# Four forget logits carried by the value matmuls of a fused two-block layer, in place of a weight tile of their own

## What is computed

```python
z = h @ w_in
qa, ka, va, qb, kb, vb, fz, gza, gzb = jnp.split(z, SPLIT_POINTS, axis=-1)
ya = dilated_mixture(qa, ka, va) @ w_up_a
yb = forgetting_attention(qb, kb, vb, fz, b_forget) @ w_up_b
merged = jax.nn.sigmoid(gza) * ya + jax.nn.sigmoid(gzb) * yb
return merged @ w_out

# in forgetting_attention: 4 heads of 64, so fz has 4 columns, beside vb's 256
log_f = jax.nn.log_sigmoid(f_logit + b_forget)
F = jnp.cumsum(log_f, axis=1).transpose(0, 2, 1)
s = q_t . k_s * Dh ** -0.5 + (F_t - F_s)      # causal softmax over s, then times v
```

## Time and profile before

| | us |
|---|---|
| median of 3 runs (1991.33 to 1991.41) | 1991.33 |
| the profiled execution | 1992.63 |
| its span, first to last instruction | 1990.9 |
| TensorE's matmuls busy | 1973.5 |
| TensorE's weight loads busy | 1655.7 |
| VectorE / ScalarE / GpSimd busy | 1018.7 / 695.1 / 406.8 |

### The profile page before, as it was taken

How to read it: one execution, slowest core, us unless ns; L and a number is a source line. 1 busy time by engine, 2 the same in 40 slices (tenths; PEclk the granted TensorE clock), 3 DMA queues, 4 the chain that set the end, 5 groups by cost and what they waited for, 6 DMA issues and landing times.

```text
span 1990.9 us, 27158 instructions
## 1 busy us (share of the span) xinstructions
PE 1973.5 (99%) x11044; PEld 1655.7 (83%) x11044; DVE 1018.7 (51%) x1391; ACT 695.1 (35%) x1008; POOL 406.8 (20%) x212
## 2 busy tenths in 40 slices
PE   8999999999999999999999999999999999999998
PEld 7878888888888888889888888888877888888887
DVE  5468757457345336626727535642544664322435
ACT  6357643122124323315312212534434352222222
POOL 1000007696600001000568661000000200000000
PEclk9999999999999999999999999999999999999999
DMA  6221134444333232222445442232221223323231
GB/s 190 79 64 44 44 117 148 158 149 147 129 106 117 73 108 85 85 102 91 156 138 169 148 134 100 85 94 81 71 85 64 86 84 106 104 98 106 84 106 64
DMA packets 135033, 208.91 MB, mean 105 GB/s; under 512 B 6347, under 2 KB 105865, under 8 KB 134921
## 3 DMA queue, kind: packets, MB, share of 16 engines
q1 hardware_dynamic: 125952, 180.37, 27.9%
q0 software_dynamic: 6912, 25.17, 3.8%
q10 hardware_dynamic: 2056, 1.76, 0.3%
HBM read 205.18 MB, written 2.10 MB: 104 GB/s over the span
## 4 chain that ended last, share of the span: by engine, by line
PE 94%; DVE 3%; ACT 2%; issue 0%; ACTq 0%
PE ps L2158 28%; PE ps L2160 28%; PE ps L2159 28%; PE ps L2219 1%; PE ps L2609 1%; PE ps L2212 1%; PE ps L2211 1%; PE ps L2620 1%; PE ps L2709 1%; PE ps L2182 1%; PE ps L2801 1%; DVE m L1466 0%; PE ps L2598 0%; PE ps L2597 0%; ACT ps L761 0%
## 5 line engine op out<-in xcount | busy, mean ns | idle before, releaser
L1388 DVE TENSOR_TENSOR w_lo<-w_raw,w_hi 128x2048 fp32r<-128x2048 f32 x149 | 350.9, 2355 | 577.0 <-ACT w_hi L726 577.0
L2158 PE MATMUL ps<-x_hi,w_hi 128*128 128x512 f32 x1240 | 489.1, 394 | 0.4 <-DVE w_lo L1388 0.4
L2160 PE MATMUL ps<-x_hi,w_lo 128*128 128x512 f32 x1240 | 483.0, 390 | 0.0
L2159 PE MATMUL ps<-x_lo,w_hi 128*128 128x512 f32 x1240 | 482.9, 389 | 0.0
L726 ACT ACTIVATE w_hi<-w_raw 128x2048 fp32r<-128x2048 f32 x151 | 288.9, 1913 | 536.1 <-PE ps L2160 435.1
L2158 PEld LDWEIGHTS ps<-x_hi,w_hi 128*128 128x128 f32 x1240 | 233.0, 188 | 51.0 <-issue 3.5
L2160 PEld LDWEIGHTS ps<-x_hi,w_lo 128*128 128x128 f32 x1240 | 232.7, 188 | 48.8
L2159 PEld LDWEIGHTS ps<-x_lo,w_hi 128*128 128x128 f32 x1240 | 233.1, 188 | 45.9
L2158 PE MATMUL ps<-w_hi,h_hi 128*128 128x512 f32 x688 | 267.8, 389 | 0.0
L2160 PE MATMUL ps<-w_hi,h_lo 128*128 128x512 f32 x688 | 267.7, 389 | 0.0
L2159 PE MATMUL ps<-w_lo,h_hi 128*128 128x512 f32 x688 | 267.7, 389 | 0.0
(11 more groups left out here) (404 smaller groups left out, 2694.2 us busy)
## 6 DMA issues: line engine op xcount, KB each, us to landing
w_raw<-in_ffn_w SPq DMA_DIRECT2D x64, 1024.0 KB, 5.4
ada_w<-in_w_ada POOLq DMA_DIRECT2D x48, 512.0 KB, 4.2
w_raw<-in_w_ffn_in SPq DMA_DIRECT2D x22, 1024.0 KB, 5.1
w_raw<-in_w_in SPq DMA_DIRECT2D x20, 1024.0 KB, 5.4
w_raw<-in_o_w_in SPq DMA_DIRECT2D x16, 1024.0 KB, 5.4
w_raw<-in_w_ffn_out SPq DMA_DIRECT2D x11, 1024.0 KB, 4.9
w_raw<-in_e_w_in SPq DMA_DIRECT2D x9, 1024.0 KB, 5.4
w_raw<-in_o_w_out SPq DMA_DIRECT2D x8, 1024.0 KB, 4.9
```

The source lines that it names most:

```text
L1388: nc.vector.tensor_tensor(w_lo[:, slot, :], w_raw[:, slot, :], w_hi[:, slot, :].bitcast(F32), ALU.subtract).then_inc(w_lo_ready, 1)
L2158: nc.tensor.matmul(dst, a_hi, b_hi, start=start, stop=False)
L2159: nc.tensor.matmul(dst, a_hi, b_lo, start=False, stop=False)
L2160: return nc.tensor.matmul(dst, a_lo, b_hi, start=False, stop=stop_)
```

## The change

The tile `s_small` and its unit are gone. The tile of the values is loaded with 260 columns instead of 256, the four of `fz` behind those of `vb`; the weight buffers are 32 columns longer for it (8 row blocks of 260 are 2080). The value matmuls have 260 moving columns. Their fill units are four of four steps (one block of 128 tokens each, six matmuls a step) instead of two of eight. ScalarE takes the 128x4 logits of each unit into `f_cols` and the 128x256 values into `v_ab`, in two instructions. In pair 4, after the first group of fill, TensorE turns the four `f_cols` tiles into free columns of banks 4 and 5 (`forget_turned`), and VectorE copies them into `f_row` with the bias at the pair's end. The logarithm moves to pair 5 on ScalarE, the sum to pair 6 and `f_two` to pair 7 on VectorE; the frame of `f_two` and `f_pick` stays in pair 1. In pair 5 `s_rows` waits for VectorE's copies. The fill has 192 steps instead of 200, so the pairs get 176 instead of 184: 5 and 6 in every pair, instead of 5 and 6 or 6 and 6. All tiles and units behind move by one tile and one unit number, which swaps the slots and the banks.

```diff
-             ("s_qk", 6, 2), ("s_va", 3, 2), ("s_small", 1, 1), ("s_qkb", 2, 2), ("s_vb", 1, 2),
+             ("s_qk", 6, 2), ("s_va", 3, 2), ("s_qkb", 2, 2), ("s_vb", 1, 4),
...
+        w_raw_all = sb("w_raw", [P, 2 * TILE + 32])
+        w_raw = w_raw_all[:, 0:2 * TILE].rearrange("p (s c) -> p s c", s=2)
...
+        f_cols = place("f_cols", [P, NT, 4], Y_ + 44)
...
+        def v_b(t):
+            return t[:, TILE:2 * TILE + 32].rearrange("p (k c) -> p k c", k=8)
...
-                return 2 if self.units[j][1] == "up" else DK
+                return {"up": 2, "straight": 4}.get(self.units[j][1], DK)
...
+        F_PAIR = 4
...
-            n = S["s_small"].first
-            load(n, n % 2, [(by8(w_raw, n % 2)[:, :, 0:P], w_s2[:, :, FZ:FZ + P])])
             load_listed("s_qkb", w_s2, [QB, KB])
-            load_listed("s_vb", w_s2, [VB])
+            load(S["s_vb"].first, 1, [(v_b(w_raw_all), w_s2[:, :, VB:VB + 260])])
...
-                if kind == "small":
-                    fa = f_row[0:4, :]
-                    nc.scalar.activation(f_tmp[0:4, :], src[32:36, :], ACT.Identity, bias=b_forget[:, 0:1]).then_inc(f_part, 1)
-                    act.wait_ge(bank_free, 4 + S["s_small"].unit + 1)
-                    chain.link(nc.scalar.activation(f_tmp[0:4, :], fa, ACT.Abs))
-                    chain.link(nc.scalar.activation(f_tmp[0:4, :], f_tmp[0:4, :], ACT.Exp, scale=-1.0))
-                    nc.scalar.activation(f_tmp[0:4, :], f_tmp[0:4, :], ACT.Ln, bias=1.0).then_inc(f_sum, 1)
...
                 elif kind == "straight":
-                    nc.scalar.activation(v_ab[:, 2 * f:2 * f + 2, 768:1024], src.rearrange("p (t c) -> p t c", t=2),
-                                         ACT.Copy).then_inc(bank_free, 1)
+                    nc.scalar.activation(f_cols[:, f, :], src[:, 256:260], ACT.Copy).then_inc(f_part, 1)
+                    nc.scalar.activation(v_ab[:, f, 768:1024], src[:, 0:256], ACT.Copy).then_inc(bank_free, 1)
...
+            def forget_logs():
+                act.wait_ge(f_copied, 2)
+                fb = f_tmp[0:4, :]
+                chain.link(nc.scalar.activation(fb, f_row[0:4, :], ACT.Abs))
+                chain.link(nc.scalar.activation(fb, fb, ACT.Exp, scale=-1.0))
+                nc.scalar.activation(fb, fb, ACT.Ln, bias=1.0).then_inc(f_sum, 1)
...
+                if pair == F_PAIR + 1:
+                    forget_logs()
...
             def forget_logits():
-                j = filler.finished(0)[0]
-                dve.wait_ge(f_part, 1)
-                nc.vector.tensor_tensor(f_row[0:4, :], ps[0:4, 6 + j % 2, :], f_tmp[0:4, :], ALU.add).then_inc(bank_free, 1)
+                dve.wait_ge(f_turned, 1)
+                for part, src in ((slice(0, 3 * P), ps[0:4, 4, P:4 * P]), (slice(3 * P, 4 * P), ps[0:4, 5, 2 * P:3 * P])):
+                    nc.vector.tensor_scalar(f_row[0:4, part], src, b_forget[:, 0:1], None, ALU.add).then_inc(f_copied, 1)
...
-            def forget_rest():
-                n = S["s_small"].first
...
                 if pair == 1:
+                    forget_frame()
+                if pair == F_PAIR + 2:
                     forget_sum()
+                if pair == F_PAIR + 3:
+                    forget_rows()
...
+                if pair == F_PAIR:
+                    forget_logits()
...
                 elif kind == "straight":
-                    for part in range(2):
-                        t, kk = 2 * f + k // 4, 2 * (k % 4) + part
-                        toks = slice(t * P, (t + 1) * P)
-                        o = mm3(ps[:, bank_, (k // 4) * 256:(k // 4) * 256 + 256], x_hi[:, kk, toks], x_lo[:, kk, toks],
+                    hi, lo, toks = v_b(w_hi_all), v_b(w_lo_all), slice(f * P, (f + 1) * P)
+                    for kk in (2 * k, 2 * k + 1):
+                        o = mm3(ps[:, bank_, 0:260], x_hi[:, kk, toks], x_lo[:, kk, toks],
                                 hi[:, kk, :], lo[:, kk, :], kk == 0, kk == DK - 1)
-                elif kind == "small":
-                    nc.tensor.matmul(ps[:, bank_, :], hi[:, k, 0:P], x_hi[:, k, :], start=(k == 0), stop=False)
-                    o = nc.tensor.matmul(ps[:, bank_, :], hi[:, k, 0:P], x_lo[:, k, :], start=False, stop=(k == DK - 1))
...
+            def forget_turned():
+                pe.wait_ge(f_part, NT)
+                pe.wait_ge(a_normed, 2 * F_PAIR)
+                pe.wait_ge(a_taken, F_PAIR)
+                for t in range(NT):
+                    dst = ps[0:4, 4, (t + 1) * P:(t + 2) * P] if t < 3 else ps[0:4, 5, 2 * P:3 * P]
+                    o = nc.tensor.transpose(dst, f_cols[:, t, :], ident[:, :])
+                o.then_inc(f_turned, 1)
...
                 if 0 < pair <= N_S // 4:
+                    if pair == F_PAIR + 1:
+                        pe.wait_ge(f_copied, 2)
                     s_rows(pair - 1)
                 for j, k in filler.during(2 * pair + 1):
                     fill(j, k)
+                if pair == F_PAIR:
+                    forget_turned()
```

More of the change, by code:

```diff
@@ L426, in __init__ @@
                 self.units = []
-                for name, kind in (("s_small", "small"), ("s_qkb", "turned"), ("s_vb", "straight"), ("s_gate", "turned"),
+                for name, kind in (("s_qkb", "turned"), ("s_vb", "straight"), ("s_gate", "turned"),
                                    ("s_upa", "up")):
@@ L433, in __init__ @@
                 self.steps = [(j, k) for j in range(len(self.units)) for k in range(self.depth(j))]
-                self.first = S["s_small"].unit
+                self.first = S["s_qkb"].unit
                 before, after = DK, (4, 4)
@@ L725, in split_hi @@
                     act.wait_ge(mm_done, used)
-                nc.scalar.activation(w_hi[:, slot, :], w_raw[:, slot, :], ACT.Copy).then_inc(w_hi_ready, 1)
+                if isinstance(n, int) and n == S["s_vb"].first:
+                    nc.scalar.activation(w_hi_all[:, TILE:], w_raw_all[:, TILE:], ACT.Copy).then_inc(w_hi_ready, 1)
+                else:
+                    nc.scalar.activation(w_hi[:, slot, :], w_raw[:, slot, :], ACT.Copy).then_inc(w_hi_ready, 1)
             def split_next(st, i, q, it):
@@ L768, in root_table @@
             def root_table():
-                nc.scalar.activation(root[:, 16:17], small[:, 22:23], ACT.Sqrt)
+                nc.scalar.activation(small[:, 23:24], small[:, 22:23], ACT.Sqrt)
             def bank_pair(t):
@@ L1240, in _ @@
             take_far(1)
-            nc.scalar.activation(root[:, 16:17], small[:, 22:23], ACT.Exp)
+            nc.scalar.activation(small[:, 23:24], small[:, 22:23], ACT.Exp)
             keep_far(3)
@@ L1293, in _ @@
             exp_scores(1)
-            n = S["s_small"].first + 1
+            n = S["s_qkb"].first + 1
             split_hi(n, n % 2, loaded(n), S["s_va"].done + 6)
@@ L1387, in split_lo @@
                 dve.wait_ge(w_hi_ready, n + 1)
+                if isinstance(n, int) and n == S["s_vb"].first:
+                    nc.vector.tensor_tensor(w_lo_all[:, TILE:], w_raw_all[:, TILE:], w_hi_all[:, TILE:].bitcast(F32),
+                                            ALU.subtract).then_inc(w_lo_ready, 1)
+                    return
                 nc.vector.tensor_tensor(w_lo[:, slot, :], w_raw[:, slot, :], w_hi[:, slot, :].bitcast(F32),
@@ L1954, in forget_logits, with forget_frame @@
             def forget_logits():
[L1955 to L1957 removed]
+                dve.wait_ge(f_turned, 1)
+                for part, src in ((slice(0, 3 * P), ps[0:4, 4, P:4 * P]), (slice(3 * P, 4 * P), ps[0:4, 5, 2 * P:3 * P])):
+                    nc.vector.tensor_scalar(f_row[0:4, part], src, b_forget[:, 0:1], None, ALU.add).then_inc(f_copied, 1)
+            def forget_frame():
+                nc.vector.tensor_tensor(f_pick[:, :], ident[:, 0:4], ident[:, 32:36], ALU.add)
+                chain.link(nc.vector.tensor_scalar(f_two[:, :], causal_row[:, :], 0.0, None, ALU.mult))
             def forget_sum():
@@ L1965, in forget_sum, with forget_rows @@
                                                         ALU.mult, ALU.add))
-                nc.vector.tensor_tensor(f_pick[:, :], ident[:, 0:4], ident[:, 32:36], ALU.add)
-                chain.link(nc.vector.tensor_scalar(f_two[:, :], causal_row[:, :], 0.0, None, ALU.mult))
+            def forget_rows():
+                fa = f_row[0:4, :]
                 chain.link(nc.vector.tensor_copy(f_two[0:4, :], fa))
@@ L1997, in take_up @@
                                                    ALU.add, ALU.mult).then_inc(upa_gated, 1)
-            forget_rest()
+            n = S["s_qkb"].first
+            split_lo(n, n % 2)
             max_scores(0)
             max_scores(1)
-            n = S["s_small"].first + 1
-            split_lo(n, n % 2)
+            split_lo(n + 1, (n + 1) % 2)
             for pair in range(N_S // 2):
-                if pair == 0:
-                    forget_logits()
                 if pair:
@@ L2879, in _ @@
             far_turn(3)
```

(2 more changed lines are left out.)

19 lines of the change are left out of this document (7 added, 12 removed).

## The result

The changed kernel takes **2025.99 us** (median of 4 runs, 2025.93 to 2026.09), the kernel before 1991.37 beside it on the same chip (4 runs, 1991.33 to 1991.55): a ratio of 1.0173, 95% interval 1.0160 to 1.0185. I had forecast 1989.5 within 1987.6 to 1991.8. It is slower by 34.6 us, far outside of the range and on the side to which I gave 0.08. The span of the profiled execution went from 1990.9 to 2024.2 us, and the granted clock of TensorE is 0.999 (its level of 2.4 GHz) in both.

A forecast was written before the change was run, and what follows sets the result against it. TensorE's instruction stream was taken as the bound (matmuls cover 99% of the span). The terms -3.65 - 0.37 + 0.16 + 0.44 + 1.51 + 0.10 gave -1.81 us, so 1991.33 becomes 1989.5 us, range 1987.6 to 1991.8.

The forecast's parts named there:

- nowhere near TensorE's path: Weight buffers: the dropped weight load and 32 extra columns per split and transfer stay off TensorE's path; no term in the sum.
- rival of a slower gait: Value matmuls of 260 columns run at the 512-column spacing, costing 10.4 us instead of 0.16: 1999.7 us, chance 0.05.
- The last sentence: Said a change outside the attention stage would be none of the listed cases and not explicable from the rows.
- other losses over 4 us: Whole kernel: any loss over 4 us other than the slower gait of 260-column matmuls, chance 0.03.
- The 16 matmuls of the logits' unit: Forget logits' unit on TensorE: 16 matmuls of 512 columns leave, -3.65 us; with the 0.37 us wait, -4.02.
- The 96 value matmuls of 260 columns: Attention stage, TensorE: four more columns cost 1.7 ns per matmul, 0.16 us in all, bounds 0 to 10.4.
- my lower bound: Value matmuls of 260 columns: 0 us, were the spacing at 256 set by something other than the columns.
- The wait for f_two: End of pair 7: TensorE's first scores of the second attention wait 1.51 us for VectorE's f_two, bounds 0 to 2.1.
- wait for a bank: Pair 2: the values' third unit waits for the bank ScalarE empties, 0.1 us, between 0 and 0.4.
- ScalarE's logarithm in pair 5: Pair 5: the moved logarithm and table loads delay the exponentials 0.9 us, covered with 1.2 us to spare.
- No wait for f_two: Pair 7: ScalarE's split comes earlier or VectorE passes it sooner, so -3.3 us, 1988.0 us; chance 0.14.
- ScalarE late: Pair 5: table loads hold ScalarE twice as long, TensorE loses 1.3 us, 1990.8 us; chance 0.13 including similar small waits.

The follow-up runs named there:

- e1: Kernel before with only the changed kernel's memory layout (weight buffers 32 columns longer, root's scratch column moved into small): 2028.06 us.
- e9: Changed kernel with small tiles re-placed so w_hi, w_lo, key_parts and big tiles lie multiples of 256 bytes from their places in the kernel before: 1989.38 us.
- e10: As e9, but VectorE makes f_two at the end of pair 6, ahead of the next weight tile's split: 1988.48 us.
- e7: Kernel before with an unused tile of 256 bytes ahead of the big tiles, all else in place: 1991.75 us.
- e11: Kernel before with w_lo alone 128 bytes out of step, every other tile a multiple of 256 bytes from its old place: 2015.15 us.
- e3: Kernel before with 64 unused bytes ahead of the big tiles, weight buffers staying: 2017.14 us.
- e8: Changed kernel with small tiles put together, so big tiles and w_lo lie at +256 bytes and w_hi at +128: 2019.64 us.

## Why the prediction was wrong, step by step

**The step that failed** is the sentence that the 32 columns which a split and a transfer gain "are nowhere near TensorE's path". It priced the longer buffers by what reads and writes the 32 columns, and had no term for what lies behind them in memory. Measured alone that term is +36.7 us (e1), twenty times the rest of the sum. With it, measured afterwards, the sum would have been 1989.5 + 36.7 = 2026.2; the run gave 2025.99. The only remark on layout was in the rival of a slower gait, of 260-column matmuls; there the row was missing and the place wrong. The last sentence, that a change outside of the stage would be none of the cases, was true: 0.03 for "other losses over 4 us" was too little for a diff that moves every tile of the program.

**The rest of the sum held.** It was -1.81 us; the instructions gave -2.07 on the changed layout (e1) and 1989.38 - 1991.52 = -2.14 with distances kept (e9). Term by term, in e9's trace where distances are those of before:

- The 16 matmuls of the logits' unit and the wait of 0.37 for w_lo are gone, as forecast (-4.02); no wait for w_lo stands in TensorE's list.
- The 96 value matmuls of 260 columns are spaced no wider than those of 256, where the forecast had 0.16 us for them. Of 35 in a row the first and the last start 4.06 us apart, 34 spacings of 0.119 us, where 256 columns took 0.120:

```profile
1416.77 0.28 PE L2175 MATMUL ps<-w_lo,x_hi 128*128 128x260 f32 x1
...
1420.83 0.28 PE L2176 MATMUL ps<-w_hi,x_lo 128*128 128x260 f32 x1
```

- Without the few at the end of a group, the mean is 119.5 ns (91 matmuls), against 119.8 for 256 columns before (92). So my lower bound was right: those four columns don't show in the spacing. I had drawn a straight line between the spacings at 256 and 512 columns, and backed it with the earlier trace rows, which are durations; a duration isn't a spacing.
- The four transposes lie 107 to 110 ns apart: 0.44, as forecast.
- The wait for f_two is 1.39 us in the changed kernel and 1.43 in e9; forecast 1.51. The timeline of the changed kernel reads as the prediction had put it together from pair 7 of before (as the earlier trace rows):

```profile
1489.80 1.04 PE L2817 MATMUL ps<-ident,s_prob 128*128 128x128 f32 x8
...
1496.83 0.49 PE L2908 MATMUL ps<-q_kb 64*128 64x128 f32 x4 [1.39 <-DVE f_two L1990]
...
1493.36 2.29 DVE L1404 TENSOR_TENSOR w_lo<-w_raw,w_hi 128x2048 fp32r<-128x2048 f32 x1 [1.56 <-ACT w_hi L736]
1495.57 0.41 DVE L1989 CAST f_two<-f_row 4x512 fp32r<-4x512 f32 x1
1496.01 0.68 DVE L1990 TENSOR_TENSOR f_two<-f_row,f_two 4x512 fp32r<-4x512 f32 x1
```

- f_two is done 1496.69 - 1489.80 = 6.89 us into the pair (forecast 7.04), and e10, which takes the cause away, takes the wait away.
- In pair 2 no wait for a bank (forecast 0.1, bounds 0 to 0.4).
- ScalarE's logarithm in pair 5 is covered. In e9's timeline its exponentials begin at 1451.11, 8.4 us into the pair (forecast 8.7), and the next pair's transposes at 1453.52 wait for nothing:

```profile
1445.58 1.28 ACT L1292 ACT_TABLE_LOAD   x1
1446.87 0.63 ACT L1292 ACTIVATE f_tmp<-f_tmp 4x512 f32<-4x512 f32 x1
...
1451.11 0.68 ACT L1262 ACTIVATE s_prob<-ps,att_stat 128x512 f32<-128x512 f32 x1
...
1453.52 1.03 PE L2817 MATMUL ps<-ident,s_prob 128*128 128x128 f32 x8
```

With these, -4.02 + 0.44 + 1.43 = -2.15, against -2.07 and -2.14 measured. Agreement to a few hundredths is luck, since one execution of the same program can differ from another by more (1991.24 to 1993.28 for the kernel before). One reading of the prediction falls for that reason: it put the 1.3 us by which the profiled execution of the kernel before exceeds the median down to profiling. That trace has one wait at the start, which the trace of e7, with the same instructions and profiled as well (1991.75 us), doesn't have:

```profile
PE ps L2173 <- DVE m L1415: 1.7, 1, 1.7
```

So the dependences were read rightly and the layout was not read at all.

**The rivals.** No wait for f_two: wrong, it came. ScalarE late: wrong. Slower gait: the spacing did get slower and did decide the case, but of matmuls of 512 columns that the diff doesn't touch, and not of those with 260.

## What to carry to other kernels

A change in a buffer's size is a change of every address behind it. Before costing the instructions of such a diff, write down where the moving and the stationary tiles start, modulo 256 bytes, before and after: in this kernel equal residues meant 227 ns a matmul of 512 columns and unequal ones up to 233 in the mean of a class, 1.2 to 2.1% of the whole program. When groups that a diff doesn't touch all grow by a few ns, run the old instructions on the new layout first: here that one run split +34.6 us into +36.7 and -2.1.

## What the runs showed of the hardware that I had not expected

- The spacing of matmuls of 512 columns (F32R tiles) depends on the distance between the start of the moving tile and that of the stationary tiles (its own, and the next one's), taken modulo 256 bytes and not modulo 128: with the big tiles 256 bytes further nothing is lost, 32 bytes cost 42.5 us over the program, 64 cost 25.7, 128 cost 38.2. A common shift of all tiles by 32 costs nothing (1991.72 against 1991.76).
- It takes both streams: one operand out of step slows the matmuls in which it is used and, as stationary tile, the one ahead (e11). Why a matmul goes on paying for its own stationary tile, whose load is over, stays open, and so do what lies behind the period and why matmuls at the same distance pay differently (e3, e8). Whether bf16 or short matmuls show the same wasn't tried; the 256-column ones whose w moves over x got no slower in any layout (120 ns in step, 115 to 120 out of step).
- 256 and 260 moving columns take 0.120 and 0.119 us from start to start, with a load of a new stationary tile ahead of each. The rows of 260 lie 1040 bytes apart, so in e9 most of them start out of step with x, and at this length it doesn't show.
